# State-space mixer: exponentials stay in their PSUM bank, and the decay steps stand in other slots

## The reference

```
def ssd_chunked(x, dt, a, bm, cm):          # 32 heads, 4 groups of 8 heads, 2 chunks of 128 tokens
    xdt = x * dt
    da  = dt * a
    cs  = cumsum(da)                        # inside a chunk
    decay  = where(lower, exp(cs_l - cs_s), 0)
    scores = (cm @ bm^T) * decay            # 128 x 128 per head and chunk
    y_diag = scores @ xdt
    ... plus the state carried from chunk 0 to chunk 1
y = (y + x * D) * silu(z); rms_norm over each group; @ w_ssd_out
```

## Time and profile before

| | |
|---|---|
| median of 3 runs | 1461.05 us (1457.92 to 1463.77) |
| profiled execution | 1458.56 us, its span 1456.7 us |
| PE busy | 1380.3 us (95%) |
| PEld busy | 1266.4 us (87%) |
| DVE busy | 1033.2 us (71%) |
| ACT busy | 893.6 us (61%) |
| POOL busy | 329.0 us (23%) |
| granted PE clock over the span | 0.988 |
| the mixer's four groups | from 729.74 us (first `ssd_cb`) to about 1020 us (last `ssd_norm`) |

### The profile page before, as it was taken

How to read it: one execution, slowest core, us unless ns; L and a number is a source line. 1 busy time by engine, 2 the same in 40 slices (tenths; PEclk the granted TensorE clock), 3 DMA queues, 4 the chain that set the end, 5 groups by cost and what they waited for, 6 DMA issues and landing times.

```text
span 1456.7 us, 29899 instructions
## 1 busy us (share of the span) xinstructions
PE 1380.3 (95%) x11462; PEld 1266.4 (87%) x11462; DVE 1033.2 (71%) x1567; ACT 893.6 (61%) x1694; POOL 329.0 (23%) x320
## 2 busy tenths in 40 slices
PE   6998999998998999999899998989899799999999
PEld 6888999997887999998788887978788699899998
DVE  6787855567577666569888999766896576566554
ACT  5455744467587555558778786767675455665443
POOL 2000411124002111125744435200500012331100
PEclk9999999999999999999999999999999899999999
DMA  8332555554932655544444443433555254355652
GB/s 321 124 117 87 177 200 200 183 195 146 200 122 99 229 192 201 191 157 157 162 145 149 142 145 120 146 120 112 174 171 174 87 174 150 111 182 195 202 186 75
DMA packets 35608, 233.80 MB, mean 161 GB/s; under 512 B 4000, under 2 KB 7072, under 8 KB 8352
## 3 DMA queue, kind: packets, MB, share of 16 engines
q1 hardware_dynamic: 31104, 223.75, 44.7%
q10 hardware_dynamic: 3216, 4.19, 1.9%
q0 software_dynamic: 1168, 4.20, 1.0%
HBM read 227.93 MB, written 4.19 MB: 159 GB/s over the span
## 4 chain that ended last, share of the span: by engine, by line
PE 49%; DVE 10%; ACT 4%; issue 3%; POOL 1%; DMA 0%; ACTq 0%; DVEq 0%; POOLq 0%
PE ps L464 7%; PE ps L465 7%; PE ps L474 7%; PE ps L533 4%; PE ps L534 4%; PE ps L539 4%; DVE w_lo L1902 3%; PE ps L872 2%; PE ps L873 2%; PE ps L876 2%; ACT w_hi L1190 2%; DVE arena L2317 1%; POOL arena L2703 1%; PE ps L516 1%; PE ps L920 1%
## 5 line engine op out<-in xcount | busy, mean ns | idle before, releaser
L1902 DVE TENSOR_TENSOR w_lo<-raw,w_hi 128x1024 bf16<-128x1024 f32 x420 | 539.8, 1287 | 253.5 <-ACT w_hi L1190 253.3
L1190 ACT CAST w_hi<-raw 128x1024 fp32r<-128x1024 f32 x420 | 438.5, 1047 | 339.0 <-PE ps L474 133.7
L464 PE MATMUL ps<-xa_both,w_hi 128*128 128x256 f32 x1296 | 324.7, 292 | 12.3 <-ACT w_hi L1190 10.7
L465 PE MATMUL ps<-xa_both,w_hi 128*128 128x256 f32 x1296 | 307.3, 279 | 0.0
L464 PEld LDWEIGHTS ps<-xa_both,w_hi 128*128 128x128 f32 x1296 | 245.8, 190 | 18.3 <-issue 12.3
L465 PEld LDWEIGHTS ps<-xa_both,w_hi 128*128 128x128 f32 x1296 | 246.1, 190 | 0.7 <-issue 0.2
L533 PE MATMUL ps<-xb_both,w_hi 128*128 128x256 f32 x832 | 204.7, 288 | 0.1
L534 PE MATMUL ps<-xb_both,w_hi 128*128 128x256 f32 x832 | 195.1, 277 | 0.0
L474 PE MATMUL ps<-xa_bf,w_lo 128*128 128x256 bf16 x1296 | 169.4, 274 | 2.0 <-DVE w_lo L1902 1.9
L872 PE MATMUL ps<-xb_both,w_hi 128*128 128x256 f32 x592 | 151.0, 296 | 7.8 <-DVE arena L2317 6.5
L533 PEld LDWEIGHTS ps<-xb_both,w_hi 128*128 128x128 f32 x832 | 156.6, 188 | 1.6 <-DVE xb_both L1917 0.3
(11 more groups left out here) (339 smaller groups left out, 2372.2 us busy)
## 6 DMA issues: line engine op xcount, KB each, us to landing
raw<-weights SPq DMA_DIRECT2D x210, 1024.0 KB, 4.9
band<-arena ACTq DMA_DIRECT2D x1, 3072.0 KB, 35.5
arena<-band POOLq DMA_DIRECT2D x8, 256.0 KB, 3.2
arena<-gla_masks SPq DMA_DIRECT2D x1, 1088.0 KB, 15.4
H<-x_t SPq DMA_DIRECT2D x2, 512.0 KB, 5.0
arena<-band POOLq DMA_DIRECT2D x8, 128.0 KB, 2.6
arena<-mem_t POOLq DMA_DIRECT2D x1, 1024.0 KB, 5.1
out_t<-H ACTq DMA_DIRECT2D x8, 128.0 KB, 2.0
```

What stands on the lines that cost most here:

```text
L464: mm(ps[:, bank, 0:T], w_hi[:, s, k], X.hi[:, k], start=k == 0, stop=False)
L465: mm(ps[:, bank, 0:T], w_hi[:, s, k], X.lo[:, k], start=False, stop=False)
L1190: nc.scalar.copy(w_hi[:, j % HI_SLOTS].rearrange("p k n -> p (k n)"), raw[:, j // 2 % RING, j % 2]).then_inc(hi_done, 1)
L1902: TT(w_lo[:, j % HI_SLOTS].rearrange("p k n -> p (k n)"), raw[:, j // 2 % RING, j % 2], w_hi[:, j % HI_SLOTS].rearrange("p k n -> p (k n)" ...
```

## The change

`ssd_exp` writes its result back into bank 5, in place, and `ssd_sc` reads it from there. `s_e` is no longer used. So bank 5 is free only after the multiply: `ssd_quad(n)` and `ssd_cb` wait for `sa["sc"]` (the multiply) where they waited for `sa["e"]` (the exponential), and `ssd_exp` loses its wait for an earlier multiply. The table of slots changes with it. The lines of the changed kernel behind L1577 have numbers 2 lower (L1580 for L1582, L2355 for L2357).

```
-    dict(cb=0, quad=(1, 3, 5, 7), turn=(2, 3), y=(6, 8, 11, 12), sums=(12, 16), exp=(1, 3, 5, 7), eb=(8, 12), squares=(10, 14),
-         xd=(2, 3), sc=(4, 5, 9, 10), combine=(9, 13), norm=8),
-    dict(cb=0, quad=(1, 3, 8, 12), turn=(2, 3), y=(6, 7, 13, 14), sums=(11, 17), exp=(1, 3, 11, 12), eb=(7, 14), squares=(9, 16),
-         xd=(2, 3), sc=(4, 5, 12, 13), combine=(8, 15), norm=5),
+    dict(cb=0, quad=(1, 3, 5, 10), turn=(2, 3), y=(6, 8, 11, 13), sums=(12, 17), exp=(1, 3, 5, 10), eb=(8, 13), squares=(10, 15),
+         xd=(2, 3), sc=(2, 4, 9, 11), combine=(9, 14), norm=8),
+    dict(cb=0, quad=(1, 3, 8, 13), turn=(2, 3), y=(6, 7, 13, 15), sums=(11, 18), exp=(1, 3, 11, 13), eb=(7, 15), squares=(9, 17),
+         xd=(2, 3), sc=(2, 4, 12, 14), combine=(8, 16), norm=5),
@@ ssd_cb (PE)
                 if g:
-                    pe.wait_ge(sa["e"], 4 * g)
+                    pe.wait_ge(sa["sc"], 4 * g)
@@ ssd_quad (PE)
                 if q or t:
-                    pe.wait_ge(sa["e"], n)
+                    pe.wait_ge(sa["sc"], n)
@@ ssd_exp (ACT)
                 act.wait_ge(sa["c"], n + 1)
-                if n >= 2:
-                    act.wait_ge(sa["sc"], n - 1)
-                    ins = A(s_e[:, n % 2, i * P:(i + 1) * P], ps[:, 5, i * P:(i + 1) * P], ACT.Exp, bias=s_small[:, 7, h:h + 1])
+                    ins = A(ps[:, 5, i * P:(i + 1) * P], ps[:, 5, i * P:(i + 1) * P], ACT.Exp, bias=s_small[:, 7, h:h + 1])
@@ ssd_sc (DVE)
-                TT(s_sc[:, n % 2].rearrange("p (h l) -> p h l", h=4), s_e[:, n % 2].rearrange("p (h l) -> p h l", h=4),
+                TT(s_sc[:, n % 2].rearrange("p (h l) -> p h l", h=4), ps[:, 5, :].rearrange("p (h l) -> p h l", h=4),
```

## The result

Four runs of the changed kernel gave a median of 1482.01 us (1479.63 to 1485.96), four of the kernel before in the same comparison 1459.49 us (1457.44 to 1463.77). The ratio is 1.0153, interval [1.0119, 1.0187]. The forecast was 1473 with a range of 1463 to 1479: the sign is right, the size too small, and the time lies outside the range. The forecast had added its 11.8 us to 1461.05, the median known then; against that the measured time is 21.0 higher. The profiled execution took 1481.0 us, its span is 1479.1 us; before it was 1458.56 and 1456.7. The granted clock (the share of its full 2.4 GHz that TensorE was given) is 0.979 over the span, before 0.988.

A forecast was written before the change was run, and what follows sets the result against it. PE sets the pace, with DVE close behind. A 3.4 + B 7.1 + C 2.5 - 5.9 + 0.5 + D 3.7 + E 0.5 = +11.8 us on 1461.05 gives 1472.9, rounded 1473; range 1463 to 1479.

The forecast's parts named there:

- The multiply: DVE's multiply, now with one operand from PSUM: 0.68 us for all 16 instead of 1132 ns; bounds 0.68 and 1.13.
- The exponential into PSUM: ACT's exponential, now writing PSUM: 0.1 us either way for one, 0.4 for four; both ends come to nothing.
- A: Second decay block, slot 3, four groups: waits for the first multiply, +0.85 us each, +3.4.
- B: Third decay block, slot 5, groups 0 to 2: PE waits 2.38 us for the second multiply, +7.1.
- R2: Rival: the second multiply comes in time for slot 5: 1462 to 1466, or 1456; chance 0.13.
- C: Fourth decay block, slot 10, groups 0 to 2: +0.83 each, +2.5; gap at slot 11 closes, -5.9; group 2 +0.5.
- D: ACT from slot 13, groups 0 to 2: two more table loads each, later squares, wider gap at slot 3: +3.7.
- The copy: ACT's copy `s_cb` after the squares: 1.6 us late with 1.0 to spare, so PE waits 0.5 for it.
- R1: Rival: the added table loads on ACT are hidden, D goes to 0: +8.1, 1469; chance 0.20.
- E: End of group 3: combine, squares and sums a slot later, half of one `ssd_sums`: +0.5, between 0 and 3.
- R3: Rival: ACT's loads cost more than 1.28, or DVE in slots 14 to 17 becomes late: +15.8, 1477; chance 0.12.
- R4: Rival: exponential into PSUM or multiply from the bank just written takes far longer: 1476 at 1.13; chance 0.05.

The follow-up runs named there:

- experiment 3: The changed kernel with the two SiLUs of slot 12 moved to slot 13 behind the exponential, so the six added table loads go: 1483.76 us, ratio 1.0159.
- experiment 1: The kernel before (exponentials into `s_e`, no block waits for a multiply) with the changed table of slots: 1466.76 us, ratio 1.0030.
- 5: The changed kernel with only the later steps (y, sums, `ssd_eb`, squares, combine) back at the slots of before: 1474.43 us, ratio 1.0104.
- experiment 6: The changed kernel with four useless 128x256 matmuls before the second `ssd_turn` and four before the third block, groups 0 to 2: 1474.29 us, ratio 1.0102.
- experiment 7: The kernel of 4 with two useless DVE copies before the first `ssd_xd` of groups 0 to 2, lengthening PE's wait at slot 3: 1462.16 us, ratio 1.0007.
- 9: The kernel of experiment 7 with four useless matmuls on PE before the second `ssd_turn`: 1459.26 us, ratio 0.9980.
- 2: The changed kernel with the third decay block and its exponential at slot 6 instead of 5, groups 0 to 2: 1470.39 us, ratio 1.0063.
- 10: The kernel of 4 with four useless matmuls before the second `ssd_turn`, without the two copies: 1456.10 us, ratio 0.9962.
- 4: The changed data path with blocks at 1, 4, 7, 10, multiplies at 2, 5, 9, 11, later steps back where they were: 1455.88 us, ratio 0.9969.
- 8: The kernel of 4 with the third multiply of groups 0 to 2 at slot 8 instead of 9: 1457.27 us, ratio 0.9977.

## Why the prediction was right in sign and too small

- **The multiply**: forecast 0.68, measured 0.68 in all 16 (0.677 to 0.685), nine of which ran beside a POOL add. The rule behind it is in the Trainium skill, "SBUF — State Buffer", section "SBUF: two separate sides": DVE's shared port is contested with GpSimd only where a DVE operation has two SBUF inputs (or is in a mode with two ports). This trace agrees: with one operand in PSUM none of the 16 was stretched, against 1132 ns in the mean before, where they took 681 to 1785 ns. The exponential into PSUM took 0.34, inside the bounds. (The forecast's price for a slow multiply, +2.7 at 1.13 us, had left out A, whose block waits for a multiply too.)
- **A**: forecast +0.85 each, 3.4. Measured 0.78, 0.83, 0.84, 0.83: 3.3.
- **B**: forecast a wait of 2.38, 7.1 in all. Measured gaps 2.21, 2.22, 2.22, shift 2.5 each, 7.6. R2, that the multiply comes in time, is refuted.
- **C**: forecast 2.5 - 5.9 + 0.5 = -2.9. Measured -2.7 without the clock: waits of 0.67, 0.67 and 1.05, no gap at slot 11.
- **D**: forecast +3.7, measured +3.9 (1.24, 1.55, 1.08), at the place that was named: the gap at slot 3. But the cause is another than half of the term had it. Not the table loads (experiment 3), but products one slot later (experiments 1 and 5). The copy had 0.2 us of wait, not 0.5. It was right by its sum, not by its working, and that is luck. R1, by which hidden loads make D nothing, falls as well: they are hidden, and D is there.
- **E**: forecast +0.5; group 3 behind its slot 3 adds 0.9 without the clock.
- **R3 and R4** put the extra in loads, in a late DVE in slots 14 to 17, or in slow PSUM access. Loads and slow access were not found. The squares do wait 1.88 us for DVE's combine, but no run separates that, and 1477 would have been too small too.

These terms sum to +13.0 where the forecast had +11.8. **The step that failed is the sum itself, which has no term for the clock**: it priced a wait by its length and took every matmul at its time of full clock. Behind the waits at slot 3 and slot 5, TensorE ran at 1.2 GHz for some us. That adds 5.2 us to the shifts of the one trace. Another 1.7 come in group 3, behind the 1.96 us before L1000 at 975.25; the kernel before waits there too (1.89 us, at 955.27) and has no drop behind it. Together 6.9 (10.2 by the second count). The experiments show it: with work put into the waits 7.7 us come back (experiment 6), and behind the same added wait PE takes 6.01 or 3.27 us to the next block according to whether it was idle or busy in it (7 and 9). The 9.1 us between 1472.9 and 1482.0 are thus, but for rounding, 6.9 of clock, 1.2 of terms a little too small, and 2.5 that lie ahead of the mixer, less 1.6 because the kernel before had a median of 1459.49 in this comparison and not 1461.05. The profile before could have raised the question, though not answered it. Its clock was 1.00 in groups 0 to 2 with gaps of up to 3.28, which I read as safe; the change put a gap of 3.1 and one of 0.2 to 0.3 within 1.4 us of each other, and another of 2.2 some 10 us on. The range should have held a rival "the clock falls behind the new waits"; its price, 1.0 to 2.8 us for each drop, could be known only from the traces after.

What stays open: the 2.5 us ahead of the mixer, in unchanged code. The trace after has 3.4 us more of withheld clock there (10.2 against 6.8). Those of experiments 1, 2, 5 and 9 have as much, those of 3, 6 and 10 have 8.5, and those of 4, 7 and 8 have 6.8. Since 9 has the table of 4 and 7 and yet 10.2, it does not hang on the table alone. Runs of the kernel before differ among themselves by more (1454.33 to 1464.95 us in 23 runs, with a granted clock of 0.992 to 0.983), so it may be chance; no run here settles it. Open is also what decides whether a given wait is followed by a drop.

## What to carry to other kernels

Where PE is the bound, price a new wait at its length and then ask what the granted clock does behind it: here three waits longer by 1.2 us cost 6.3 us with PE idle and 3.2 with useless matmuls in them. A result written back in place ties the producer's next step to the consumer, so move the steps until the consumer is done before the bound engine arrives; the same data path was 1.5% slower than before with one table and 0.3% faster with another. And test a term's cause even when its sum comes out right, as D did here for the wrong reason.

## What the runs showed of the hardware that was not expected

- Waits of the same length are followed by half clock in one place or run and not in another: 3.28 us alone with 1.00 behind it (before), 1.78 and 0.67 with 1.00 (after, group 0) and with 0.60 (experiment 3, group 0).
- A drop, once there, withholds 1.7 or 3.4 us of clock: the stretch behind 816 us 4 x 0.43 = 1.7, those from 884 to 896 us 0.1 + 2.0 + 1.3 = 3.4. It delays PE by less: 1.0 and 2.5 us by the shifts of groups 1 and 2 from slot 3 to slot 5 (3.57 and 5.04, less the 2.54 of group 0), and 1.5 to 2.8 in experiment 7.
- The same program runs with and without drops: of the twelve executions of experiment 1, four had a granted clock of 0.986 to 0.987 (1460.7 to 1462.5 us), eight 0.981 to 0.985 (1465.3 to 1467.9 us).
- Adding 24 matmuls that compute nothing made a kernel 7.7 us faster.
- The exponential was 27 ns faster into PSUM (341) than into SBUF (368). The Trainium skill, "ScalarE: Activation LUTs", section "Step-by-step: what each stage is for", has ScalarE's way to PSUM as the shorter one, and the two groups agree with it.
